# Projecting the values of the dilated groups from consecutive tokens and moving their halves to the group's order by DMA

## What is computed

```python
ATTN_GROUPS = ((128, 1), (512, 4), (2048, 16))     # (window, dilation)
xn = rms_norm(h, attn_norm_w[l])
z = xn @ w_in[l]                                   # q | k | v | glu | memory q | gates
v = zv.reshape(B, S, N_GROUPS, HEADS_PER_GROUP, HEAD_DIM)
for g, (win, dil) in enumerate(ATTN_GROUPS):
    # query t attends to the keys t - j*dilation, j = 0..win//dilation
    o_g, lse_g = dilated_window_attention(q[:, :, g], k[:, :, g], v[:, :, g], cols, win, dil)
wts = jax.nn.softmax(jnp.stack(lses), axis=0)
attn = jnp.sum(wts[..., None] * jnp.stack(outs), axis=0)
```

## Time and profile before

| | |
|---|---|
| median of 3 runs | 1873.53 us (1870.85 to 1874.79) |
| the profiled execution | 1873.44 us, of which its span is 1871.6 us |
| PE busy | 1847.9 us, 99% |
| PE weight loads busy | 1573.2 us, 84% |
| DVE / ACT / POOL busy | 1202.8 (64%) / 772.2 (41%) / 86.7 us (5%) |
| TensorE's granted clock | the upper level throughout (mean 0.999 of full speed) |
| DMA | 186.45 MB, mean 100 GB/s |

### The profile page before, as it was taken

How to read it: one execution, slowest core, us unless ns; L and a number is a source line. 1 busy time by engine, 2 the same in 40 slices (tenths; PEclk the granted TensorE clock), 3 DMA queues, 4 the chain that set the end, 5 groups by cost and what they waited for, 6 DMA issues and landing times. The chain is left out here.

```text
span 1871.6 us, 23740 instructions
## 1 busy us (share of the span) xinstructions
PE 1847.9 (99%) x8778; PEld 1573.2 (84%) x8778; DVE 1202.8 (64%) x1681; ACT 772.2 (41%) x1420; POOL 86.7 (5%) x150
## 2 busy tenths in 40 slices
PE   7999999999999999999999999999999999999999
PEld 6788889989998888888888888887888888878887
DVE  5535763674372788996425616478787878767675
ACT  6423542453253155213523322365454545444443
POOL 1101110111010010000000000000000000000000
PEclk9999999999999999999999999999999999999999
DMA  7432433132333101102113415112222232267543
GB/s 256 168 119 68 136 113 101 50 126 96 102 108 111 52 2 46 46 23 68 46 33 98 151 37 180 57 57 90 79 84 84 73 95 67 84 211 265 160 141 102
DMA packets 135377, 186.45 MB, mean 100 GB/s; under 512 B 15925, under 2 KB 64437, under 8 KB 135285
## 3 DMA queue, kind: packets, MB, share of 16 engines
q1 hardware_dynamic: 126979, 174.53, 28.7%
q10 hardware_dynamic: 8306, 10.68, 1.6%
HBM read 145.21 MB, written 42.32 MB: 100 GB/s over the span
## 5 line engine op out<-in xcount | busy, mean ns | idle before, releaser
L240 PE MATMUL psum<-whi,act_lo 128*128 128x512 f32 x768 | 312.3, 407 | 2.8 <-DVE q_lo L553 0.9
L242 PE MATMUL psum<-whi,act_hi 128*128 128x512 f32 x768 | 302.9, 394 | 0.0
L241 PE MATMUL psum<-wlo,act_hi 128*128 128x512 f32 x768 | 302.7, 394 | 0.0
L240 PE MATMUL psum<-act_hi,wlo 128*128 128x512 f32 x512 | 202.2, 395 | 0.0
L242 PE MATMUL psum<-act_hi,whi 128*128 128x512 f32 x512 | 199.6, 390 | 0.0
L241 PE MATMUL psum<-act_lo,whi 128*128 128x512 f32 x512 | 199.3, 389 | 0.0
L240 PEld LDWEIGHTS psum<-whi,act_lo 128*128 128x128 f32 x768 | 178.0, 232 | 23.2 <-DVE wlo L198 2.2
L242 PEld LDWEIGHTS psum<-whi,act_hi 128*128 128x128 f32 x768 | 178.0, 232 | 20.5
L241 PEld LDWEIGHTS psum<-wlo,act_hi 128*128 128x128 f32 x768 | 178.8, 233 | 17.6
L193 ACT CAST whi<-stage 128x512 fp32r<-128x512 f32 x200 | 120.0, 622 | 172.5 <-PE psum L242 165.8
L198 DVE TENSOR_TENSOR wlo<-stage,whi 128x512 fp32r<-128x512 f32 x200 | 129.9, 687 | 93.0 <-ACT whi L193 92.2
(11 more groups left out here) (252 smaller groups left out, 3518.9 us busy)
## 6 DMA issues: line engine op xcount, KB each, us to landing
stage<-in_w_in SPq DMA_DIRECT2D x144, 256.0 KB, 4.0
u_raw<-in_w_up SPq DMA_DIRECT2D x44, 512.0 KB, 5.0
stage<-in_w_down SPq DMA_DIRECT2D x44, 256.0 KB, 3.7
w_sums<-stage SPq DMA_DIRECT2D x44, 256.0 KB, 2.5
gated_scratch<-g_buf SPq DMA_DIRECT2D x22, 512.0 KB, 2.7
gated<-gated_scratch SPq DMA_DIRECT2D x44, 256.0 KB, 3.9
d_raw<-w_sums SPq DMA_DIRECT2D x44, 256.0 KB, 2.7
d_raw<-in_w_down SPq DMA_DIRECT2D x33, 256.0 KB, 3.3
```

The costliest lines, as they stand in the source:

```text
L240: nc.tensor.matmul(dst, lhs[1], rhs[0], start=first, stop=False, skip_group_check=True)
L241: nc.tensor.matmul(dst, lhs[0], rhs[1], start=False, stop=False, skip_group_check=True)
L242: return nc.tensor.matmul(dst, lhs[0], rhs[0], start=False, stop=last, skip_group_check=True)
```

## The change

V tiles take 128 tokens in a row in every group (`act_tile`). In group 0 that is what they did. In groups 1 and 2 the two halves now go to a buffer `v_stage` of two tiles, laid over `pt_hi` and `pt_lo`, and one step later ACT issues DMAs from it into `v_both`: 4 of 32 partitions each in group 1, 8 of 16 partitions each in group 2, each with 4 KB per partition (both halves). The move of tile t-1 is issued behind the values' cast of tile t. From the third V tile of group 1 on, a cast waits until the tile's half of the buffer has been moved out. Before the first product with the values of a group, PE and ACT wait for all moves.

```diff
+        v_stage = at("v_stage", off + 12288, [2, 2, CW], F32R)
...
-                self.lhs = act_tile(slice(t * P, (t + 1) * P)) if kind in "KX" else group_tile(g, t)
+                self.lhs = act_tile(slice(t * P, (t + 1) * P)) if kind in "KVX" else group_tile(g, t)
...
+        v_moved = [sem("v_moved_even"), sem("v_moved_odd")]
+
+        def moves_before(g, t):
+
+            return sum(16 * (1, 4, 8)[g2] for g2 in range(1, min(g, NG - 1) + 1) for t2 in range(t % 2, NT, 2) if g2 < g or t2 < t)
+
+        def value_tile(part, tl):
+            return v_stage[:, tl.t % 2, part, :] if tl.g else vT[part][:, tl.t, :]
+
+        def move_values(act, tl):
+
+            r = (1, 4, 8)[tl.g]
+            rows = P // r
+            per_class = S // r
+            act.wait_ge(gemm_freed, tl.index + 1)
+            for c in range(r):
+                tile, p0 = divmod(c * per_class + tl.t * rows, P)
+                act.dma_start(v_both[p0:p0 + rows, :, tile, :].bitcast(F32),
+                              v_stage[c:P:r, tl.t % 2, :, :].bitcast(F32)).then_inc(v_moved[tl.t % 2], 16)
...
# tiles_pe, before the first product with the values
+                    if tl.kind == "Q" and tl.g and tl.t == 0:
+                        for j in range(2):
+                            pe.wait_ge(v_moved[j], moves_before(tl.g + 1, j))
...
# tiles_act, in the step of tile i and behind it
-                        values_hi(act, tl.v, tl.index, vT[0][:, tl.t, :])
+                        if tl.g and tl.t >= 2 or tl.g >= 2:
+                            act.wait_ge(v_moved[tl.t % 2], moves_before(tl.g, tl.t))
+                        values_hi(act, tl.v, tl.index, value_tile(0, tl))
...
+                tl = tile_of(part, i - 1, "V")
+                if tl and tl.g:
+                    move_values(act, tl)
...
# tiles_act, before the first copy into pt
+                    if tl.kind == "Q" and tl.g and tl.t == 0:
+                        for j in range(2):
+                            act.wait_ge(v_moved[j], moves_before(tl.g + 1, j))
...
-                        values_lo(dve, tl.v, tl.index, vT[0][:, tl.t, :], vT[1][:, tl.t, :])
+                        values_lo(dve, tl.v, tl.index, value_tile(0, tl), value_tile(1, tl))
```

## The result

The changed kernel takes 1885.49 us (median of 6 runs, 1884.8 to 1888.91) against 1871.68 us for the kernel before on the same chip (6 runs): a ratio of 1.0071, 95% interval 1.0061 to 1.0081, so 13.8 us slower. The forecast was 1875.3 us with a range up to 1884.8. It started from 1873.44 us for the kernel before, 1.8 us above the median of the six runs here; in differences it forecast 1.9 us slower. The profiled execution took 1884.8 us, its span 1883.0 us.

The account below looks back on a forecast made before the run. PE was taken to bound the kernel, busy 99% of the span. From 1873.44 us, 5.0 gained, 5.9 added by group 2's moves and 1.0 by other traffic gave 1875.3 us; the 8-in-10 range was 1867.8 to 1884.8.

Parts of the forecast that it names:

- other traffic: SP's stores and loads during group 2's V tiles delay the moves: 1 us taken, between nothing and 7 us.
- five distances beyond 5.44: Group 2's value casts 2 to 7 slip 1.26 us each past PE's 5.44 us a tile: 6.3 us late.
- end of the turn: After group 2's V tiles, the next weights' casts and subtractions leave 0.4 us of the 6.3 covered; 5.9 reach PE.
- The gain: V tiles of groups 1 and 2 read tokens in a row: 1.6 us and 3.4 us saved, 5.0 us together.
- C in group 2: Time from a value cast to the landing of the last move issued behind it: 1.5 + 5.2 = 6.7 us.
- X: Time 512 KB of moves take: 5.2 us in group 2, at a quarter of the full rate, chosen between two ends.
- Group 1: Time from cast to last landing there is 4.1 us, under PE's 5.44: moves hidden with 1.3 us of cover.
- a slip of casts in group 1: Sign of a wrong prediction: value casts slipping in group 1 too, where the moves were forecast as hidden.
- The cover inside the V tiles: In group 2, 4.1 us of cast slip is covered before PE wants the tile's bank.
- hidden: Rival: group 2's moves land in 5.0 us, the whole gain stays, 1868.4 us (to 1870.5); chance 0.28.
- Partitions set the rate: Rival: few partitions limit the moves, 10.3 us for 512 KB in group 2; 1903.9 us (1885 to 1905); chance 0.12.
- Doesn't do what it says: Rival: V tiles keep their pace, something other than the block's step set it; about 1878 us; chance 0.05.

Follow-up runs that it names:

- the rate experiment: Changed kernel with two DMAs a tile instead of eight (four), same 512 KB into the same 16 (32) neighbouring partitions: 1881.06 us.
- e7_one_narrow: Changed kernel with two DMAs a tile instead of eight (four), same bytes into the same neighbouring partitions, each half row repeated: 1881.06 us.
- e2_four_tiles: Changed kernel with a `v_stage` buffer of four tiles instead of two: 1871.26 us, ratio 0.9992 to the kernel before.
- e3_sp_small: Changed kernel with SP's four stores, four loads and bias load during group 2's V tiles cut to 8 columns each: 1880.8 us.
- e13_tiny_moves: Changed kernel with the same 96 moves cut to 8 columns of each half, 64 bytes per partition: 1874.96 us.

## Why the prediction was wrong

The sum was 1873.44 - 5.0 + 5.9 + 1.0. The place and the order of the events were right, and group 2's moves did cost more than they gain; the size was not right. The step that failed is the term of 1.0 us for other traffic, which measured 7.9 us; the issue time behind two other terms was also too small. In group 2, against the kernel without moves:

| term in us | forecast | measured |
|---|---|---|
| five distances beyond 5.44, without SP's traffic | 6.3 | 7.2 |
| other traffic | 1.0 | 7.9 |
| end of the turn | -0.4 | 3.0 |
| together | 6.9 | 18.1 |

- **The gain**: right. Loads at 188 ns, 32.6 us for six tiles, 6.5 us without moves (its interval holds 5.0).
- **C in group 2**: 6.7 us forecast, 6.87 measured, so the distance was right partly by luck. X was chosen as 5.2 us; the rate experiment shows about 4 us for 512 KB, but a distance of 6.6, so 2.6 us around the data instead of 1.5. At the same time the issues made a loop of 6.3 us where I had reckoned 5.3 to 5.8, because I took an issue at 0.44 us from DMAs between SBUF and DRAM. It takes 0.61 to 0.64.
- **Group 1**: its balance was forecast at a gain of 1.6 us and came out even. Three issues of 0.65 us and a landing of 3.3 to 3.4 us make C 5.4 to 5.5 us instead of 4.1, so no cover was left for SP's transfers (6.5 us of waiting at the cast of 310.86). Casts slipped there and PE waited 0.8 us before the first query tile; the prediction had named a slip of casts in group 1 as a sign of being wrong.
- **Other traffic: the step that failed most.** I took 1 us, near the lower end of 0 to 7, because a stream at a quarter of the rate would leave the engines room. The two distances were 2.2 and 5.6 us longer than 6.87, so 7.9 us, beyond the upper end. Without SP's bytes 7.1 us of slip are gone. Undisturbed, the moves do leave room: the DMA share reads 0.26 to 0.44 from 453 to 458 us. But once moves queue up they don't: at 96 to 106 GB/s in `e7_one_narrow` the share reads 0.96 to 1.04, and in `e2_four_tiles` from 484 to 486 us, where nothing of SP's is moving, the moves that have piled up fill it (1.09) at some 125 GB/s. Beside SP's transfers the changed kernel's moves land after 4.5 to 7.9 us instead of 2.4, and in a closed loop every microsecond of it comes through.
- **The cover inside the V tiles**: right. The cast at 474.81 is 6.6 us late, and PE waits 2.65 us for its bank, near the 2.5 that the forecast's cover of 4.1 us leaves. The slip of 15.1 us in place of 6.3 used the cover up, so 7.8 us of waiting fell inside the V tiles, where the forecast counted none.
- **The end of the turn**: forecast as covered by 0.4 us, measured as 3.0 over the kernel without moves. The longer issues are 1.6 of it (5.1 for 3.5 us ahead of the weights' casts).
- **TensorE's clock**: in no term. Behind the wait of 3.9 us the clock is at the lower level, matmuls start every 0.43 us instead of 0.23, and eight such are 1.7 us more at the turn's end. With the longer issues that is 3.3 us, less the cover of 0.4, so 2.9 of the 3.0 measured. The slower matmuls inside the V tiles (4.4 us) fall where the casts wait for moves anyway; that they cost nothing of their own is argued, not shown.
- **The rivals**: "hidden" fell with the issues of 0.64 us. "Partitions set the rate" was right as a mechanism in group 2 (spread destinations, twice the rate) at a quarter of the full rate, not an eighth. Its interval of 1885 to 1905 holds the measured time by luck: it wanted distances of 11.8 us from the moves alone, and they were 6.87. "Doesn't do what it says" fell with the gain.
- **The range**: its upper end counted 7 us of other traffic with a C of 7.4 us. The measured other traffic and turn's end come to 10.9 us where that end had 6.6, more than its longer C made up for. The kernel before, 1.8 us faster in the median than in the profiled execution from which I started, brought the measured time nearer to the range, by luck.

## What to carry to other kernels

A transfer in a loop closed by a small buffer is priced as issues, plus data, plus one landing, plus whatever other queues send meanwhile, and all of it counts once the sum passes the pace of the engine it feeds. Where rows must change partitions, one wide store to DRAM and wide loads in the new order can cost less than many narrow transfers inside SBUF, since the order is then chosen on the DRAM side (19.5 us less here). When two limits lie close together, taking away one shows little: measure each with the other one gone.

## What the runs showed of the hardware

- Issuing a DMA on ACT's queue took 0.33 us for the stores of `ob` and `v_dram` from SBUF to DRAM, 0.46 for that of `softstat`, and 0.61 to 0.64 from SBUF to SBUF when undisturbed, with 16, 32 or 128 partitions and 1 to 512 KB.
- 512 KB into 16 neighbouring partitions settled at 96 to 106 GB/s, into every eighth partition at 160 to 211; into 32 neighbouring partitions they came down from 158 to 88 and took about 4 us, as into 16.
- Issues stretch when SP's transfers run: eight took 7.16 us instead of 5.08 in the changed kernel, and 6.03 with moves of 1 KB.
- Moves of 64 KB landed 2.4 to 2.5 us after their issue alone, and 4.5 to 7.9 us beside SP's transfers. Undisturbed they kept the DMA engines busy for 0.26 to 0.44 of the time; piled up, in `e2_four_tiles`, for all of it at some 125 GB/s.
- Behind waits of 2.65 to 5.1 us TensorE ran at 1.2 GHz for some 3 to 5 us (eight to thirteen matmuls in each case of the changed kernel); behind single waits of 1.1 (`e3_sp_small`) to 2.35 us (`e13_tiny_moves`) it did not.
